# Residual norms: squares summed as moving columns into one row, in place of token-column products

## The chip, the cores and the metric

One Trainium2 chip, of which the kernel uses one core. The metric is device time in microseconds (us) of one execution. The engines are TensorE (PE in the views; PEld is its weight load), VectorE (DVE), ScalarE (ACT), GpSimd (POOL) and SyncE (SP), which issues the DMAs. Each runs its own instruction stream, and they are ordered by semaphores.

## The reference, cut to what matters

Two blocks of two layers each work on a residual stream x of width 1024, with 512 latent tokens and, in the first block's first layer, 256 context tokens beside them. Each layer part starts with an RMS norm over the 1024 channels of a token:

```
def rmsnorm(x, g):
    xf = x.astype(jnp.float32)
    y = xf * lax.rsqrt(jnp.mean(xf * xf, axis=-1, keepdims=True) + EPS)
    return (y * g).astype(x.dtype)

xl = xl + ml[2] * rmsnorm(yl, norm_mix_post[layer])
hl = modulate(rmsnorm(xl, norm_ffn_pre[layer]), ml[3], ml[4])
xl = xl + ml[5] * rmsnorm(conv_ffn(hl, ...), norm_ffn_post[layer])
```

The sum of squares of x for the second line is what is computed in another way here. The mixers (gated recurrences, mLSTM, gated delta rule), the convolutions and the feed-forward products stay as they are.

## The kernel before

x is held with the channels on the 128 partitions, as eight parts `xT[:, k, :]` of up to 768 token columns (256 context, then 512 latent; `LATENT` stands for the latter alone, `BOTH` for the two segments). A sum over channels is therefore a sum over partitions, which TensorE makes.

Each engine's stream is written by hand, in the order in which it runs; semaphores (`signal(...)`) tie the streams together. Around one residual norm this happens:

- VectorE (`add_normed_dve`, L553) scales the branch output y and adds it to x, part by part: L558 and L561 alternate.
- ScalarE (`x_square_act`, L530) squares each finished part of x into `hT` (L533).
- TensorE (`x_norm_pe`, L518) waits for a square and calls `token_sums_pe` (L493): for each group c of 128 tokens the 128x128 square is the stationary operand and one column of ones moves (L497). The result is one PSUM column of 128 tokens for each k, 48 columns for six groups.
- VectorE (`norm_roots_dve`, L542) reduces the eight columns of a group to one (L547), scales and adds EPS (L548); ScalarE takes the root (L528); VectorE inverts (L550).
- TensorE (`norm_spread_pe`, L501) spreads the columns over all partitions with an identity product (L505), into `RT` in PSUM.
- VectorE multiplies x by `RT` (L569, in the delta layer L2581), ScalarE makes the high part of the split operand (L581 or L2404), VectorE the low part (L572), and the next weight products (L357, L1815) start.

The columns of y's norm are made by the same `token_sums_pe`, with n = 2, and are not touched. `x_norm_pe` is called in four places: before the first feed-forward block and before the mLSTM block (BOTH, six groups), before the second feed-forward block and before the first delta block (LATENT, four groups). The second delta layer and the final norm make their sums with `x_sum_pe` inside `join_pe`; these stay.

Two other things are queued at these places. At the first two POOL starts splitting weight blocks into high and low parts (L327, L328) once VectorE has added the last part of x. At the last two ScalarE and VectorE split blocks themselves (L1840, L1845), which stand in VectorE's stream ahead of the norm; before the mLSTM block VectorE has the modulation vectors (L706 to L708) there.

Of the kernel before, what the change touches and what calls it, by code (L numbers as in the profile page):

```python
# [9 lines left out]
ALU = mybir.AluOpType  # L10
ACT = mybir.ActivationFunctionType
AX = mybir.AxisListType.X

P = 128
D = 1024
KD = D // P
# [4 lines left out]
EPS = 1e-6  # L21
# [127 lines left out]
def program(nc, A, out):  # L149

    with ExitStack() as ctx:
        build(nc, A, out, ctx)

def build(nc, A, out, ctx):
    SIGNALS.clear()
    V, S, G, M = nc.vector, nc.scalar, nc.gpsimd, nc.tensor

    def signal(name):
        q = Signal(ctx.enter_context(nc.semaphore(name)))  # L160
        q.label = name
        SIGNALS.append(q)
        return q
# [26 lines left out]
    hT = h_all[:, :].rearrange("p (k t) -> p k t", k=KD)  # L190
    hlT = h_low[:, :].rearrange("p (k t) -> p k t", k=KD)
    ones, ident, halves, ident64 = gen[:, 0:P], gen[:, P:2 * P], gen[:, 2 * P:3 * P], gen[:, 3 * P:3 * P + 64]
# [35 lines left out]
    psum = [banks[:, 512 * i:512 * i + 512] for i in range(8)]  # L228
# [12 lines left out]
    def cols(name, at=0, n=1):  # L241
        return vec[:, COL[name] + at:COL[name] + at + n]

    BOTH = [(0, CTX), (CTX, LAT)]
    LATENT = [(CTX, LAT)]
# [13 lines left out]
    sum_ready = signal("sums_ready")  # L259
    ms_ready = signal("mean_squares_ready")  # L260
# [3 lines left out]
    dve_step = signal("dve_step")  # L264
# [17 lines left out]
    def link(e, step, ins):  # L282

        ins.then_inc(step.sem, 1)
        e.wait_ge(step)
# [200 lines left out]
    x_squared, cols_ready, rt_spread = signal("x_squared"), signal("norm_columns_ready"), signal("norm_spread")  # L486
# [3 lines left out]
    def extent(segs):  # L490
        return segs[0][0], segs[-1][0] + segs[-1][1]

    def token_sums_pe(pe, k, n, t, segs):  # L493

        lo, hi = extent(segs)
        for c in range(lo // P, hi // P):
            ins = M.matmul(psum[4][:, n * c + k:n * c + k + 1], t[:, P * c:P * c + P], ones[:, 0:1], start=True, stop=True)  # L497
        if k == n - 1:
            ins.then_inc(sum_ready.sem, 1)

    def norm_spread_pe(pe, segs):  # L501
        lo, hi = extent(segs)
        pe.wait_ge(cols_ready)
        for c in range(lo // P, hi // P):
            ins = M.matmul(RT[:, P * c:P * c + P], norm_cols[:, c:c + 1].to_broadcast([P, P]), ident, start=True, stop=True)  # L505
        ins.then_inc(rt_spread.sem, 1)
# [7 lines left out]
    def x_sum_pe(pe, k, segs):  # L514
        pe.wait_ge(x_squared)
        token_sums_pe(pe, k, KD, hT[:, k, :], segs)

    def x_norm_pe(pe, segs):  # L518
        for k in range(KD):
            x_sum_pe(pe, k, segs)  # L520
        norm_spread_pe(pe, segs)

    def norm_root_act(act, segs):
        lo, hi = extent(segs)
        S.activation(spare, ones[:, 0:1], ACT.Sqrt)
        act.wait_ge(ms_ready)
        t = norm_cols[:, lo // P:hi // P]
        S.activation(t, t, ACT.Sqrt).then_inc(root_ready.sem, 1)  # L528
# [6 lines left out]
    def x_norm_act(act, segs, between=None):  # L535
# [3 lines left out]
            between()  # L539
        norm_root_act(act, segs)  # L540

    def norm_roots_dve(dve, segs, n):  # L542
        lo, hi = extent(segs)
        a, b = lo // P, hi // P
        t = norm_cols[:, a:b]
        dve.wait_ge(sum_ready)
        link(dve, dve_step, V.tensor_reduce(t, psum[4][:, n * a:n * b].rearrange("p (c k) -> p c k", k=n), AX, ALU.add))  # L547
        V.tensor_scalar(t, t, 1.0 / D, EPS, ALU.mult, ALU.add).then_inc(ms_ready.sem, 1)  # L548
        dve.wait_ge(root_ready)
        V.reciprocal(t, t).then_inc(cols_ready.sem, 1)  # L550
        dve.wait_ge(rt_spread)
# [11 lines left out]

    def prenorm_split_dve(dve, segs, high):
        lo, hi = extent(segs)
        norm_roots_dve(dve, segs, KD)
        for k in range(KD + 1):
            if k < KD:
                V.tensor_tensor(hT[:, k, lo:hi], xT[:, k, lo:hi], RT[:, lo:hi], ALU.mult).then_inc(scaled.sem, 1)  # L569
            if k:  # L570
                dve.wait_ge(to_dve)
                V.tensor_tensor(hlT[:, k - 1, lo:hi], hT[:, k - 1, lo:hi], high[:, k - 1, lo:hi].bitcast(F32),  # L572
                                ALU.subtract).then_inc(h_ready.sem, 1)
# [2001 lines left out]
        val_used.skip(act, 2)  # L2575

    def delta_prenorm_dve(dve, l):
        norm_roots_dve(dve, LATENT, KD)
        for k in range(KD + 1):
            if k < KD:  # L2580
                V.scalar_tensor_tensor(hT[:, k, CTX:T], xT[:, k, CTX:T], cols("norm_w", 8 * l + k), RT[:, CTX:T],  # L2581
                                       ALU.mult, ALU.mult).then_inc(to_act.sem, 1)
            if k:
                dve.wait_ge(to_dve)
                V.tensor_tensor(hl_d[:, k - 1, :], hT[:, k - 1, CTX:T], hh_d[:, k - 1, :].bitcast(F32), ALU.subtract)                    .then_inc(h_ready.sem, 1)  # L2585
# [736 lines left out]
    def _(e):  # L3322
# [17 lines left out]
        phase(pe)  # L3340
        norm_spread_pe(pe, BOTH)
        x_norm_pe(pe, BOTH)
        ffn_pe(pe, 0, BOTH)
        full_down_pe(pe)
# [275 lines left out]
```

## Time and profile before

| | us |
|---|---|
| median of 3 runs | 3460.76 |
| lowest, highest | 3458.69, 3464.58 |
| the profiled execution | 3454.87 |
| its span | 3453.1 |
| PE busy | 3150.2 (91%) |
| PE weight loads busy | 2617.6 (76%) |
| DVE busy | 1926.2 (56%) |
| ACT busy | 1170.8 (34%) |
| POOL busy | 319.7 (9%) |

The page of the profile gives busy times and the costliest groups.
### The profile page before, as it was taken

The page shows a single profiled execution, that of the slowest core. Times are in us where ns is not written, and L with a number is a line of the kernel's source. Part 1 is how long each engine was busy: PE and PEld are TensorE (multiplying, and loading weights), DVE is VectorE, ACT ScalarE, POOL GpSimd, SP SyncE. Part 2 cuts the span into 40 slices and gives each one's busy share as a digit, 9 for nine tenths or more (in the row PEclk, how much of TensorE's full clock was granted, in tenths as well). Part 3 has the DMA queues.
Part 4 walks back from the last instruction along what each step waited for, and adds up shares of the span by engine and source line. Part 5 has one row for each costly group of instructions (what it writes and reads, how often), then busy time and mean ns, then how long its engine had stood idle before and what let it go on. Part 6 is the DMA issues. An engine that isn't in the chain of part 4 may idle for free. (4 is left out here: it accounts for less than half of the span.)

```text
span 3453.1 us, 69128 instructions
## 1 busy us (share of the span) xinstructions
PE 3150.2 (91%) x30200; PEld 2617.6 (76%) x30200; DVE 1926.2 (56%) x3106; ACT 1170.8 (34%) x2171; POOL 319.7 (9%) x196
## 2 busy tenths in 40 slices
PE   4999799978999989988897899999988999988898
PEld 1777488867888877776796788787777777878777
DVE  3134645453677741243278588625766854766854
ACT  2111344434222231223333433324435243525442
POOL 1232000001344400032000000000000000000000
PEclk6999899987999999889798899998989999989999
DMA  7563000020111111111000122231210222210122
GB/s 265 186 231 115 2 4 5 5 81 31 61 61 61 67 55 61 54 41 63 1 1 7 57 96 93 90 104 62 74 38 4 74 92 75 80 50 4 56 86 80
DMA packets 62760, 230.30 MB, mean 67 GB/s; under 512 B 7456, under 2 KB 7968, under 8 KB 62240
## 3 DMA queue, kind: packets, MB, share of 16 engines
q1 hardware_dynamic: 62496, 226.36, 19.0%
q8 instruction: 217, 3.56, 0.4%
q14 instruction: 47, 0.39, 0.0%
HBM read 224.24 MB, written 2.10 MB: 66 GB/s over the span
## 5 line engine op out<-in xcount | busy, mean ns | idle before, releaser
L1787 DVE SCALAR_TENSOR_TENSOR arena<-arena,vec 128x512 f32<-128x512 f32 (+1 forms) x220 | 203.3, 941 | 25.5 <-DVE arena L1785 0.2
L357 PE MATMUL bank<-h_high_ffn,w_high_ffn 128*128 128x256 f32 x704 | 183.4, 343 | 9.6 <-DVE h_low L572 9.4
L2425 DVE SCALAR_TENSOR_TENSOR x_all<-arena,vec,x_all 128x512 f32<-128x512 f32 x240 | 180.0, 750 | 10.4 <-ACT arena L2535 3.7
L357 PE MATMUL bank<-h_low,w_high_ffn 128*128 128x256 f32 x704 | 181.8, 340 | 0.0
L1845 DVE TENSOR_TENSOR ring_low<-ring,w_high_ffn 128x1024 fp32r<-128x1024 f32 x84 | 102.5, 1224 | 141.4 <-ACT w_high_ffn L1840 138.4
L357 PE MATMUL bank<-h_high_ffn,ring_low 128*128 128x256 f32 x704 | 179.9, 336 | 0.0
L357 PE MATMUL bank<-h_high_d,w_high_d 128*128 128x512 f32 x384 | 156.9, 409 | 6.4 <-DVE h_low_d L2585 6.4
L357 PE MATMUL bank<-h_low_d,w_high_d 128*128 128x512 f32 x384 | 152.9, 398 | 0.0
L357 PE MATMUL bank<-h_high_d,ring_low 128*128 128x512 f32 x384 | 152.5, 397 | 0.0
L357 PEld LDWEIGHTS bank<-h_high_ffn,w_high_ffn 128*128 128x128 f32 x704 | 132.4, 189 | 26.4 <-DVE h_low L572 7.5
L1897 DVE SCALAR_TENSOR_TENSOR arena<-arena,vec 128x512 f32<-128x512 f32 x176 | 132.4, 752 | 30.7 <-ACT arena L1858 25.3
L357 PEld LDWEIGHTS bank<-h_low,w_high_ffn 128*128 128x128 f32 x704 | 135.1, 192 | 14.8
L1815 PE MATMUL bank<-h_high_ffn,w_high_ffn 128*128 128x512 f32 x352 | 140.9, 400 | 4.9 <-DVE h_low L572 4.9
L357 PEld LDWEIGHTS bank<-h_high_ffn,ring_low 128*128 128x128 f32 x704 | 133.3, 189 | 15.4
L357 PE MATMUL bank<-h_high_b,w_high_b 128*128 128x512 f32 x320 | 130.6, 408 | 10.3 <-DVE h_low L3122 5.2
L1845 DVE TENSOR_TENSOR ring_low<-ring,w_high_b 128x1024 fp32r<-128x1024 f32 x72 | 87.9, 1223 | 92.7 <-ACT w_high_b L1840 92.4
L1817 PE MATMUL bank<-h_high_ffn,ring_low 128*128 128x512 f32 x352 | 139.6, 397 | 0.0
L1816 PE MATMUL bank<-h_low,w_high_ffn 128*128 128x512 f32 x352 | 139.1, 395 | 0.0
L357 PE MATMUL bank<-h_high_b,ring_low 128*128 128x512 f32 x320 | 128.0, 400 | 0.0
L357 PE MATMUL bank<-h_low,w_high_b 128*128 128x512 f32 x320 | 127.4, 398 | 0.0
L1840 ACT ACTIVATE w_high_ffn<-ring 128x1024 fp32r<-128x1024 f32 x84 | 88.3, 1056 | 114.0 <-DMA ring<-in_ffn_down_dram 111.9
L1350 DVE COPY_PREDICATED x_all<-arena,bank 128x256 f32<-128x256 uint32 x120 | 53.5, 446 | 128.0 <-PE bank L1104 128.0
(572 smaller groups left out, 8070.4 us busy)
## 6 DMA issues: line engine op xcount, KB each, us to landing
arena<-in_ada_w_dram SPq DMA_DIRECT2D x96, 512.0 KB, 5.5
ring<-in_ffn_up_dram SPq DMA_DIRECT2D x88, 512.0 KB, 3.3
ring<-in_d_branch_dram SPq DMA_DIRECT2D x56, 512.0 KB, 3.3
ring<-in_ffn_down_dram SPq DMA_DIRECT2D x48, 512.0 KB, 3.3
ring<-in_d_in_dram SPq DMA_DIRECT2D x32, 512.0 KB, 3.3
ring<-in_ab_in_dram SPq DMA_DIRECT2D x19, 512.0 KB, 7.2
ring<-in_c_in_dram SPq DMA_DIRECT2D x17, 512.0 KB, 3.3
ring<-in_d_join_dram SPq DMA_DIRECT2D x16, 512.0 KB, 3.3
```

The costliest lines, as they stand in the source:

```text
L357: ins = M.matmul(bank_of(tile % 2, seg), w[:, at], x(k, seg), start=first, stop=last)
L1350: V.copy_predicated(X[:, 2 * s:2 * s + 2].rearrange("p j h t -> p h j t"), level_mask[lv].unsqueeze(1).unsqueeze(1).to_broadcast([P, 2, 2, ...
L1787: ins = V.scalar_tensor_tensor(y, a, w(dy, dx), y, ALU.mult, ALU.add)
L1815: M.matmul(bank, wh[:, at], xh, start=k == 0, stop=False)
L1816: M.matmul(bank, wh[:, at], xl, start=False, stop=False)
L1817: ins = M.matmul(bank, wl[:, at], xh, start=False, stop=k == KD - 1)
L1840: S.activation(high[slot], ring[slot][:, :], ACT.Identity).then_inc(w_high_ready.sem, 1)
L1845: V.tensor_tensor(ring_low[slot][:, :], ring[slot][:, :], high[slot].bitcast(F32), ALU.subtract)\
L1897: ins = V.scalar_tensor_tensor(y, grid_at(t % 2, dy, dx), cols("ffn_conv", KF * (9 + 3 * dy + dx) + t), y, ALU.mult, ALU.add)
L2425: ins = V.scalar_tensor_tensor(y, halves2(cpad[i][:, tap:tap + LAT]), w, y, ALU.mult, ALU.add)
```

## The change

In `x_norm_pe` the square becomes the moving operand. The stationary operand is one column of ones, so the result is one row of up to 768 sums on partition 0, accumulated in PSUM over the eight parts: 256 context columns in bank 4, 512 latent columns in bank 5. VectorE copies this row into SBUF (`x_row`, partition 0 of the first square, which is no longer needed). TensorE then turns it to token columns: for each group of 128 tokens one product with the 1x128 piece of the row as stationary operand and a single 1 moving. `norm_roots_dve` is called with n = 1, so that the reduction over k falls away and the scaling reads PSUM. This adds two semaphore steps: VectorE waits for the row sums before the copy, and TensorE waits for the copy.

```
     def x_norm_pe(pe, segs):
+        lo, hi = extent(segs)
         for k in range(KD):
-            x_sum_pe(pe, k, segs)
+            pe.wait_ge(x_squared)
+            for seg in segs:
+                ins = M.matmul(x_row_banks(seg), ones[:, 0:1], hT[:, k, seg[0]:seg[0] + seg[1]], start=k == 0, stop=k == KD - 1)
+        ins.then_inc(sum_ready.sem, 1)
+        pe.wait_ge(row_ready)
+        for c in range(lo // P, hi // P):
+            ins = M.matmul(psum[4][:, c:c + 1], x_row[:, P * c:P * c + P], ones[0:1, 0:1], start=True, stop=True)
+        ins.then_inc(sum_ready.sem, 1)
         norm_spread_pe(pe, segs)
...
+    def x_row_dve(dve, segs):
+        dve.wait_ge(sum_ready)
+        for seg in segs:
+            ins = V.tensor_copy(x_row[:, seg[0]:seg[0] + seg[1]], x_row_banks(seg))
+        ins.then_inc(row_ready.sem, 1)
...
-        link(dve, dve_step, V.tensor_reduce(t, psum[4][:, n * a:n * b].rearrange("p (c k) -> p c k", k=n), AX, ALU.add))
-        V.tensor_scalar(t, t, 1.0 / D, EPS, ALU.mult, ALU.add).then_inc(ms_ready.sem, 1)
+        sums = psum[4][:, n * a:n * b]
+        if n > 1:
+            link(dve, dve_step, V.tensor_reduce(t, sums.rearrange("p (c k) -> p c k", k=n), AX, ALU.add))
+            sums = t
+        V.tensor_scalar(t, sums, 1.0 / D, EPS, ALU.mult, ALU.add).then_inc(ms_ready.sem, 1)
...
     def prenorm_split_dve(dve, segs, high):
         lo, hi = extent(segs)
-        norm_roots_dve(dve, segs, KD)
+        x_row_dve(dve, segs)
+        norm_roots_dve(dve, segs, 1)
...
     def delta_prenorm_dve(dve, l):
-        norm_roots_dve(dve, LATENT, KD)
+        if not l:
+            x_row_dve(dve, LATENT)
+        norm_roots_dve(dve, LATENT, KD if l else 1)
```

TensorE's stream before the first feed-forward block, as it was (out<-in, then the output's shape and how many in a row; `gen` holds the ones and the identity, `h_all` the squares):

```order
L497 MATMUL bank<-gen,arena 128x1 x12
L505 MATMUL bank<-gen,small 128x128 x6
L497 MATMUL bank<-gen,h_all 128x1 x48
L505 MATMUL bank<-gen,small 128x128 x6
L357 MATMUL bank<-h_high_ffn,w_high_ffn 128x256
```

And as it is with the change; a pair of 256 and 512 columns stands eight times (L527 are the row sums, L531 the turn to columns):

```order
L497 MATMUL bank<-gen,arena 128x1 x12
L505 MATMUL bank<-gen,small 128x128 x6
L527 MATMUL bank<-h_all,gen 1x256
L527 MATMUL bank<-h_all,gen 1x512
...
L527 MATMUL bank<-h_all,gen 1x256
L527 MATMUL bank<-h_all,gen 1x512
L531 MATMUL bank<-gen,h_all 128x1 x6
L505 MATMUL bank<-gen,small 128x128 x6
L357 MATMUL bank<-h_high_ffn,w_high_ffn 128x256
```

48 products with one moving column became 16 with 256 or 512, and six with one column stand behind them, after the wait for the copy.

VectorE's stream before the second feed-forward block, as it was (L1845 are the low parts of two weight blocks):

```order
L561 TENSOR_TENSOR x_all<-x_all,arena 128x512 x2
L1845 TENSOR_TENSOR ring_low<-ring,w_high_ffn 128x1024 x2
L547 TENSOR_REDUCE small<-bank 128x4
L548 TENSOR_SCALAR small<-small 128x4
L550 RECIPROCAL small<-small 128x4
L569 TENSOR_TENSOR h_all<-x_all,bank 128x512 x2
```

And with the change, where the same lines have other numbers (L582, L1867, L569, L571, L591) and L557 is the copy:

```order
L582 TENSOR_TENSOR x_all<-x_all,arena 128x512 x2
L1867 TENSOR_TENSOR ring_low<-ring,w_high_ffn 128x1024 x2
L557 COPY h_all<-bank 1x512
L569 TENSOR_SCALAR small<-bank 128x4
L571 RECIPROCAL small<-small 128x4
L591 TENSOR_TENSOR h_all<-x_all,bank 128x512 x2
```

The reduction is gone, and the copy, for which TensorE now waits, stands behind the weight splits.

## Rows read from the trace of the kernel before

**Rows 1.** Timeline, place A: start us, us, engine line op out<-in [idle before<-releaser]

```profile
821.06 20.64 PE L497 MATMUL bank<-gen,h_all 128*128 128x1 f32 x96 [3.65 <-ACT h_all L533]
...
830.56 1.71 ACT L533 ACTIVATE h_all<-x_all 128x768 f32<-128x768 f32 x2 [0.89 <-DVE x_all L561]
...
841.61 1.05 POOL L327 TENSOR_SCALAR w_high_ffn<-ring 128x1024 fp32r<-128x1024 f32 x1
841.73 0.21 DVE L547 TENSOR_REDUCE small<-bank 128x6 f32<-128x48 f32 x1 [10.33 <-PE bank L497]
841.98 0.71 DVE L548 TENSOR_SCALAR small<-small 128x6 f32<-128x6 f32 x1
...
843.21 2.93 PE L505 MATMUL bank<-gen,small 128*128 128x128 f32 x12 [1.51 <-DVE small L550]
846.18 1.82 DVE L569 TENSOR_TENSOR h_all<-x_all,bank 128x768 f32<-128x768 f32 x2 [3.02 <-PE bank L505]
```

**Rows 2.** Timeline, place B, before the mLSTM block

```profile
1451.44 20.64 PE L497 MATMUL bank<-gen,h_all 128*128 128x1 f32 x96 [3.65 <-ACT h_all L533]
...
1465.18 1.02 DVE L708 TENSOR_TENSOR modv<-mods,vec 128x16 f32<-128x16 f32 x1
...
1476.60 1.82 DVE L569 TENSOR_TENSOR h_all<-x_all,bank 128x768 f32<-128x768 f32 x2 [3.02 <-PE bank L505]
```

**Rows 3.** Timeline, place C, before the second feed-forward block

```profile
1941.63 13.81 PE L497 MATMUL bank<-gen,h_all 128*128 128x1 f32 x64 [2.64 <-ACT h_all L533]
...
1950.35 2.36 DVE L1845 TENSOR_TENSOR ring_low<-ring,w_high_ffn 128x1024 fp32r<-128x1024 f32 x2 [1.64 <-ACT w_high_ffn L1840]
...
1955.70 0.17 DVE L548 TENSOR_SCALAR small<-small 128x4 f32<-128x4 f32 x1
...
1956.38 2.08 PE L505 MATMUL bank<-gen,small 128*128 128x128 f32 x8 [0.94 <-DVE small L550]
1958.49 1.29 DVE L569 TENSOR_TENSOR h_all<-x_all,bank 128x512 f32<-128x512 f32 x2 [2.17 <-PE bank L505]
```

**Rows 4.** Timeline, place D, before the first delta block

```profile
2350.26 13.82 PE L497 MATMUL bank<-gen,h_all 128*128 128x1 f32 x64 [2.64 <-ACT h_all L533]
...
2358.99 1.23 DVE L1845 TENSOR_TENSOR ring_low<-ring,w_high_d 128x1024 fp32r<-128x1024 f32 x1 [1.65 <-ACT w_high_d L1840]
...
2367.13 1.41 DVE L2581 SCALAR_TENSOR_TENSOR h_all<-x_all,vec,bank 128x512 f32<-128x512 f32 x2 [2.17 <-PE bank L505]
```

**Rows 5.** Windows: busy us (records) of each engine, then PEclk, DMA share, GB/s

```profile
821.00:841.70 20.70, 20.64 (x96) 20.55 (x96) 10.40 (x12) 6.00 (x9) 11.53 (x7) 0.50 0.00 0
...
851.00:857.00 6.00, 5.85 (x17) 4.25 (x18) 4.29 (x6) 6.00 (x11) 0.00 (x0) 0.50 0.01 3
857.00:863.00 6.00, 3.40 (x17) 2.28 (x16) 4.85 (x6) 6.00 (x11) 0.00 (x0) 1.00 0.00 0
```

**Rows 6.** Timeline of the program's first norm (L468), products and weight loads

```profile
14.46 11.95 PE L468 MATMUL bank<-h_all,gen 128*128 128x256 f32 x32 [14.46 <-ACT h_all L458]
...
15.45 1.92 PE L468 MATMUL bank<-h_all,gen 128*128 128x512 f32 x2
...
19.37 0.19 PEld L468 LDWEIGHTS bank<-h_all,gen 128*128 128x128 f32 x1 [0.24 <-issue]
...
20.66 0.19 PEld L468 LDWEIGHTS bank<-h_all,gen 128*128 128x128 f32 x1 [0.24 <-issue]
```

**Rows 7.** Timeline and source lines: small products, spreads, a PSUM read

```profile
811.39 2.73 PE L497 MATMUL bank<-gen,arena 128*128 128x1 f32 x24
...
815.21 2.19 PE L505 MATMUL bank<-gen,small 128*128 128x128 f32 x12 [1.09 <-DVE small L550]
...
1444.89 2.90 PE L505 MATMUL bank<-gen,small 128*128 128x128 f32 x12 [1.34 <-DVE small L550]
...
26.45 1.02 DVE L475 TENSOR_SCALAR arena<-bank 128x256 f32<-128x256 f32 x2 [12.71 <-PE bank L468]
...
L2022 PEld LDWEIGHTS bank<-gen,arena x48: 285/330/335, 1679.0 to 1689.0; 64*128 64x128 f32 x48
```

More of the change, by code:

```diff
@@ L516, in x_sum_pe @@
         token_sums_pe(pe, k, KD, hT[:, k, :], segs)
+    x_row_banks = lambda seg: psum[4][0:1, 256:256 + seg[1]] if seg[0] == 0 else psum[5][0:1, 0:seg[1]]
+    x_row = hT[0:1, 0, :]
+    row_ready = signal("norm_row_ready")
     def x_norm_pe(pe, segs):
+        lo, hi = extent(segs)
         for k in range(KD):
-            x_sum_pe(pe, k, segs)
+            pe.wait_ge(x_squared)
[6 more added lines that the diff above has]
+        ins.then_inc(sum_ready.sem, 1)
         norm_spread_pe(pe, segs)
```

## The prediction

> **What bounds the kernel now.** The change touches only the sum of squares of the residual rows in four places, so I read those four places in the timeline, in order of time, and ask at each what the first use of the finished norm waits for. I call them A (before the first feed-forward block), B (before the mLSTM block), C (before the second feed-forward block) and D (before the first delta block). A and B work on all 768 token columns, C and D on 512.
>
> At A [rows 1] ScalarE squares eight parts of x; the last two squares start at 830.56 and end at 832.27 us. TensorE takes the first square at 821.06 and is busy for 20.64 us, to 841.70, with 96 records. In this trace an f32 product stands as two records, so these are 48 token-column products. TensorE thus ends 9.4 us after its last input. VectorE starts its reduction at 841.73, and the first multiplication with the finished norm starts at 846.18. So TensorE is what ends last at A, not the adds on VectorE or the squares. B is the same picture: 20.64 us from 1451.44, first use at 1476.60 [rows 2]. C takes 13.81 us from 1941.63, to 1955.44 (first use 1958.49) [rows 3], D 13.82 us from 2350.26, to 2364.08 (first use 2367.13) [rows 4].
>
> The reason is in the granted clock. Through 821 to 841.7 it is 0.50, that is the 1.2 GHz level, though TensorE is busy without a break [rows 5]. 20.64 us over 96 records is 0.215 us a record and 2.58 us a part of six products. The squares come faster: TensorE takes the first at 821.06 and the seventh ends at 831.41, six steps of 1.73 us. At full clock the same kind of product costs 2.73/24 = 0.114 us a record [rows 7].
>
> **The change, part by part.**
>
> *Sums.* Per part of 768 columns six products with a 128-column weight load and one moving column go; two products with 256 and 512 moving columns and one stationary column come. No row has one stationary column. The nearest one is the first norm of the program, which streams the same squares, 256 and 512 columns, through a 128-column matrix of ones [rows 6]. A part starts each 20.66 − 19.37 = 1.29 us there, at the full clock; at half of it 2.58 us, and two 512-column records, two thirds of a part, did take 1.92 us with their drain at the start (15.45). A smaller weight load can only take off what shows of loads, which is little where the loads run beneath the products, so I take both figures as they are; for 512 columns 1.72 and 0.86 us.
>
> So at the low clock nothing is gained: 2.58 us both ways. All of it hangs on whether the clock comes back while the row sums run. Before it rose, TensorE did this: in the first norm, some 3 us of these streaming products (32 records took 11.95 us where eight parts of 1.29 are 10.3; 1.6 us too long is 3.3 us at half speed); and 6 us of split products with 256 and 512 columns, from 851 to 857 [rows 5, 6]. It did not rise for the one-column products at A (20.64 us), nor at B, C and D, nor for 10 us of small products from 1679.0 to 1689.0, whose weight loads took 0.33 us in the median against 0.19 us at full clock [rows 6, 7]. The new products are of the first kind in what they stream. I take 4.5 us, the middle of 3 and 6.
>
> At A then: 4.5 us at 2.58 is 1.7 parts, the other 6.3 parts at 1.29 need 8.1 us, which gives 833.7; but the last two squares end at 831.41 and 832.27, and two parts behind the first of these give 834.0. With 6 us: 2.3 parts, then 5.7 × 1.29 = 7.3, so 834.4. The sum ends at 834.0 to 834.4 instead of 841.70. At B, by the same offsets, at 1464.4; but VectorE is in the modulation vectors until 1466.20 [rows 2], so its copy starts there. At C: 4.5 us is 2.6 parts, 5.4 × 0.86 more gives 1950.8 (with 6 us 1951.5), and VectorE has two weight splits ahead of the copy, to 1950.35 + 2.36 = 1952.71 [rows 3]. At D 2359.4 (2360.1), VectorE free at 2358.99 + 1.23 = 2360.22 [rows 4]. So at B, C and D what is late next is VectorE's own queue, and at A it is the squares.
>
> *The row to columns.* New on the path behind the sums: VectorE copies 256 and 512 elements of one partition (a pair of PSUM reads of that length took 1.02 us [rows 7]; I take 1.02, and two thirds, 0.68, for 512 alone), TensorE makes six (four) small products, and a reduction of 0.21 us goes. The small products load 128 columns of one row each. The nearest rows are the one-column products of 128 rows, 0.215 us a record at the low clock and 0.114 at the full one; those of 64 rows are no cheaper (48 records from 1679.0 to 1689.0 are 0.21 us each). So 12 records are 1.4 to 2.7 us with the drain, 8 records 0.95 to 1.8 us.
>
> *The root.* From the scaling on VectorE to the first spreading product 0.68 us (1955.70 to 1956.38 [rows 3]). At A and B the scaling took 0.71 us where it takes 0.17 at C: it ended with the POOL operation of 841.61 to 842.66, while the reduction before it, which reads PSUM, took 0.21 beside the same operation [rows 1]. The new scaling reads PSUM, so I take 0.17, which gives back 0.54 us each at A and B. The Trainium skill, VectorE: DVE Perf Modes, section Why PSUM operands drop a tier, says that a PSUM operand keeps an instruction out of the mode that uses both SBUF read ports; by it the new scaling and the copies would have no port to wait for, and the trace agrees as far as the 0.21 us beside 0.71 goes.
>
> *The spread.* Unchanged work: 2.19 us at full clock (815.21), 2.93 at the low one (843.21), 2.08 us for eight records at the low one [rows 1, 3, 7].
>
> Handing over costs about 0.04 us each. From the start of the copy to the first use, all at the low clock: A and B 1.06 + 2.7 + 0.68 + 2.93 + 0.04 = 7.4 us; C and D 0.72 + 1.8 + 0.04 + 0.68 + 2.08 + 0.04 = 5.36 us. All at the full clock: A, B 5.4 us; C, D 0.72 + 0.95 + 0.72 + 1.46 (8/12 of 2.19) + 0.04 = 3.9 us. Which level: after a pause of 1.3 us the spread ran at full clock at 815.21, and at the low one at 1444.89 (2.90 us) [rows 7]. At A only the copy lies between, so I take the small products at full and the spread at the low clock, 6.2 us; at B, C and D TensorE has been idle for two to three microseconds, so the low one.
>
> - A: 834.1 + 6.2 = 840.3 against 846.18: 5.9 gained (4.4 to 6.8).
> - B: 1466.2 + 7.4 = 1473.6 against 1476.60: 3.0 (to 5.0).
> - C: 1952.71 + 5.36 = 1958.1 against 1958.49: 0.4 (to 1.9).
> - D: 2360.22 + 5.36 = 2365.6 against 2367.13: 1.5 (to 3.0).
>
> Sum 10.8 us, ends 9.3 and 16.7. Behind the first use everything is paced by the same VectorE and ScalarE steps as before, then by TensorE, so it passes on whole. POOL's splits are not moved: they start with a signal that the change leaves where it is, and the last of four is under way at 841.61, ahead of the products that need it. No DMA is moved. The new wait of TensorE for the copied row has only the small products and the spread behind it, which need it anyway.
>
> The profiled execution took 3454.87 us (span 3453.1), 5.9 below the median 3460.76 of the runs. The gain is a difference of stretches, so I take it off the median: 3450.0 us.
>
> **The rivals.**
>
> *Slower: the clock stays low under the row sums.* One stationary column is something no row shows, and the one-column products show that a busy TensorE alone is not enough. Then the sums end where they end now (eight parts at 2.58 are 20.6 us), and the copy and the small products come on top: A 841.7 + 7.4 = 849.1, 3.0 later; B 1472.1 + 7.4 = 1479.5, 2.9 later; C 1955.44 + 5.4 = 1960.8, 2.3 later; D 2364.08 + 5.4 = 2369.5, 2.3 later: 10.5 us lost, 3471.3. Where it decides: with r us at the low clock the sums at A end at 821.06 + 10.32 + r/2, and A breaks even at 838.8, that is for r near 15. Against it: both streaming stretches had the full clock within some 6 us. 0.18.
>
> *Level: back at A and B only, or delayed by POOL.* C and D have shorter stretches. If the clock rises only at A and B, 8.9 − 4.6 = 4.3 us are gained, 3456.5. Or the copies do wait for POOL: a VectorE operation on 128x16 elements took 1.02 us at 1465.18 while POOL was splitting [rows 2], and three such waits at A and B, 0.9 us each, take 5.4 us of the 10.8, 3455.4. 0.12.
>
> *The change does nothing here* would need the sums to be off the path. At A they end 9.4 us after the last square and the next instruction starts 0.03 us later; I leave nothing for it.
>
> **How the numbers follow.** Forecast 0.70, level 0.12, slower 0.18. Within 0.2% is within 6.9 us, about what a measurement of this kernel can tell from no change. The forecast's ends, 9.3 and 16.7, are both beyond it: faster 0.70, same 0.12, slower 0.18. The range goes from 3443 (all at the full clock, 3444.1) to 3461 (the level cases and the runs' own spread of 3 us); left out is the slower case, 0.18.
>
> **What would show each step.** The row sums at A end near 834, with granted clock 1.00 before 828; parts 1.29 us apart or waiting for a square afterwards. At B the copy starts at 1466 less what A gained, at C directly behind the two weight splits. The two copies take about 1 us, the 12 small records 1.4 to 2.7 us, the scaling 0.17 us. Wrong if the clock is 0.50 to the end of the sums, if the small products take over 3 us, or if the copies last as long as POOL's operations beside them.

## The result, and the profile after

| | us | ratio to before (95% interval) |
|---|---|---|
| before, median of 4 runs beside it | 3459.73 (3456.08 to 3464.58) | |
| with the change, median of 4 runs | 3436.96 (3433.41 to 3438.49) | 0.9935 (0.9922 to 0.9947) |
| forecast | 3450.0 (3443 to 3461) | |

The change made the kernel faster by 22.8 us in this comparison. The direction and the mechanism are those of the forecast; the size is not: 10.8 us were forecast, and the time fell below the range. Two later comparisons of the same two kernels, with more runs, gave 0.9951 (0.9938 to 0.9965) and 0.9943 (0.9925 to 0.9962). The runs of before that stood beside others and those with the change (72 and 18 over all comparisons) have medians of 3457.4 and 3437.9 us and means of 3456.85 and 3438.15 us: about 18.7 us. The 0.9935 of the first comparison lies just outside the interval of the second and inside that of the third.

The page of the profile after the change, its first line and its busy times (of the whole execution, each engine's share of the span in brackets):

```profile
span 3435.7 us, 68762 instructions
PE 3125.1 (91%) x30016; PEld 2554.7 (74%) x30016; DVE 1926.3 (56%) x3108; ACT 1171.0 (34%) x2171; POOL 320.7 (9%) x196
```

TensorE is busy 25 us less than in the table of before and its weight loads 63 us less; the other engines are as before. Now the places. At A, the answer to [rows 1], in the timeline (start us, us, engine line op out<-in, and in brackets the idle time before it and what ended it):

```profile
826.49 6.78 PE L527 MATMUL bank<-h_all,gen 128*1 128x256 f32 x16 [3.66 <-ACT h_all L545]
...
833.42 1.45 PE L527 MATMUL bank<-h_all,gen 128*1 128x256 f32 x4 [0.15 <-ACT h_all L545]
...
835.99 1.71 ACT L545 ACTIVATE h_all<-x_all 128x768 f32<-128x768 f32 x2 [0.89 <-DVE x_all L582]
836.89 2.74 PE L527 MATMUL bank<-h_all,gen 128*1 128x256 f32 x8 [0.28 <-ACT h_all L545]
...
839.67 1.01 DVE L557 COPY h_all<-bank 1x256 f32<-1x256 f32 x2 [2.84 <-PE bank L527]
840.12 1.04 POOL L327 TENSOR_SCALAR w_high_ffn<-ring 128x1024 fp32r<-128x1024 f32 x1
...
840.73 1.49 PE L531 MATMUL bank<-gen,h_all 1*128 1x1 f32 x12 [1.10 <-DVE h_all L557]
...
842.26 0.16 DVE L569 TENSOR_SCALAR small<-bank 128x6 f32<-128x6 f32 x1 [1.59 <-PE bank L531]
...
842.95 2.80 PE L505 MATMUL bank<-gen,small 128*128 128x128 f32 x12 [0.72 <-DVE small L571]
...
845.78 1.82 DVE L591 TENSOR_TENSOR h_all<-x_all,bank 128x768 f32<-128x768 f32 x2 [2.89 <-PE bank L505]
```

Windows of the same stretch (each engine's busy us and records in the order PE, PEld, DVE, ACT, POOL, then PEclk), beside [rows 5]:

```profile
826.50:829.00 2.50, 2.50 (x4) 0.41 (x5) 2.50 (x4) 0.84 (x1) 0.00 (x0) 0.50 0.00 0
829.00:830.00 1.00, 1.00 (x4) 0.32 (x3) 1.00 (x3) 0.84 (x1) 0.00 (x0) 0.77 0.00 0
830.00:832.00 2.00, 2.00 (x7) 0.50 (x6) 2.00 (x3) 0.84 (x1) 0.00 (x0) 1.00 0.00 0
...
842.00:844.00 2.00, 1.28 (x8) 1.20 (x8) 0.36 (x2) 0.21 (x1) 2.00 (x2) 0.78 0.00 0
844.00:846.00 2.00, 1.75 (x9) 1.45 (x7) 0.22 (x1) 0.00 (x0) 1.92 (x2) 0.50 0.00 0
```

Read them together. The row sums start at the low clock, and within 829 to 830 the granted clock goes to 1.00, 3.0 us after their start. Over the four places and three profiled executions it rose 2.9 to 5.5 us after the start, latest at C (4.1 to 5.5 us). From 833.42 on TensorE waits for each square ("<-ACT h_all L545") and needs 1.45 us, with its drain, for a part that comes every 1.73 us. It ends at 839.63, which is 1.93 us behind the last square (835.99 + 1.71 = 837.70) instead of 9.4. In the brackets the releaser of TensorE has become ScalarE: that is what "the bound has moved" looks like in a timeline.

Places B, C and D, the answers to [rows 2], [rows 3] and [rows 4]; first B:

```profile
1465.40 1.00 DVE L557 COPY h_all<-bank 1x256 f32<-1x256 f32 x2
...
1466.45 1.55 PE L531 MATMUL bank<-gen,h_all 1*128 1x1 f32 x12 [2.59 <-DVE h_all L557]
1467.86 1.04 POOL L327 TENSOR_SCALAR w_high_m<-ring 128x1024 fp32r<-128x1024 f32 x1
1468.04 0.17 DVE L569 TENSOR_SCALAR small<-bank 128x6 f32<-128x6 f32 x1 [1.64 <-PE bank L531]
...
1468.73 2.93 PE L505 MATMUL bank<-gen,small 128*128 128x128 f32 x12 [0.72 <-DVE small L571]
```

C, where the copy stands behind two weight splits:

```profile
1934.67 9.08 PE L527 MATMUL bank<-h_all,gen 128*1 128x512 f32 x16 [2.64 <-ACT h_all L545]
...
1943.40 2.36 DVE L1867 TENSOR_TENSOR ring_low<-ring,w_high_ffn 128x1024 fp32r<-128x1024 f32 x2 [1.64 <-ACT w_high_ffn L1862]
...
1945.68 0.67 DVE L557 COPY h_all<-bank 1x512 f32<-1x512 f32 x1
...
1946.40 1.05 PE L531 MATMUL bank<-gen,h_all 1*128 1x1 f32 x8 [2.65 <-DVE h_all L557]
...
1948.16 1.30 PE L505 MATMUL bank<-gen,small 128*128 128x128 f32 x8 [0.71 <-DVE small L571]
1949.49 1.29 DVE L591 TENSOR_TENSOR h_all<-x_all,bank 128x512 f32<-128x512 f32 x2 [1.39 <-PE bank L505]
```

And D:

```profile
2349.99 0.67 DVE L557 COPY h_all<-bank 1x512 f32<-1x512 f32 x1
2350.71 1.05 PE L531 MATMUL bank<-gen,h_all 1*128 1x1 f32 x8 [1.17 <-DVE h_all L557]
...
2352.47 2.08 PE L505 MATMUL bank<-gen,small 128*128 128x128 f32 x8 [0.71 <-DVE small L571]
```

None of the three copies has an idle time in brackets: VectorE had no pause before them, it came to them from its own queue. TensorE had then been idle for 2.59, 2.65 and 1.17 us.

From here on I measure every profiled execution in the same way. The stretch of a norm runs from the start of the first sum on TensorE to VectorE's first use of the finished norm (where unused products hold up the first sum, from where it would start, 0.05 us behind the end of the first square); "rest" is the span without the four stretches.

| kernel (profiled span) | A | B | C | D | four together | rest |
|---|---|---|---|---|---|---|
| before (3453.1) | 25.12 | 25.15 | 16.87 | 16.87 | 84.0 | 3369.1 |
| before, again (3452.7) | 25.06 | 25.11 | 16.87 | 16.87 | 83.9 | 3368.8 |
| with the change (3435.7) | 19.29 | 20.96 | 14.82 | 14.47 | 69.5 | 3366.2 |
| with the change, again (3437.4) | 18.59 | 21.37 | 15.97 | 14.69 | 70.6 | 3366.8 |
| with the change, third (3438.1) | 18.29 | 21.22 | 15.93 | 14.62 | 70.1 | 3368.0 |

So the four stretches gave 13.4 to 14.5 us in three executions. That is the part which the change explains directly.

### The profile page after: what moved, and what is told of

It reads as the page before. It is cut to its first block and busy times, and to the rows that moved or that the text cites. A ratio compares the mean times of both kernels' runs of the same rounds, so it can differ in the third digit from the quotient of the medians.

```text
span 3435.7 us, 68762 instructions
## 1 busy us (share of the span) xinstructions
PE 3125.1 (91%) x30016; PEld 2554.7 (74%) x30016; DVE 1926.3 (56%) x3108; ACT 1171.0 (34%) x2171; POOL 320.7 (9%) x196
## 5 line engine op out<-in xcount | busy, mean ns | idle before, releaser
L357 PE MATMUL bank<-h_high_ffn,w_high_ffn 128*128 128x256 f32 x704 | 178.9, 335 | 10.8 <-DVE h_low L594 10.6
L1867 DVE TENSOR_TENSOR ring_low<-ring,w_high_ffn 128x1024 fp32r<-128x1024 f32 x84 | 102.6, 1224 | 142.1 <-ACT w_high_ffn L1862 139.2
L1867 DVE TENSOR_TENSOR ring_low<-ring,w_high_b 128x1024 fp32r<-128x1024 f32 x72 | 87.9, 1223 | 92.8 <-ACT w_high_b L1862 92.4
```

Source lines behind the costliest of these rows:

```text
L357: ins = M.matmul(bank_of(tile % 2, seg), w[:, at], x(k, seg), start=first, stop=last)
L1867: V.tensor_tensor(ring_low[slot][:, :], ring[slot][:, :], high[slot].bitcast(F32), ALU.subtract)\
```

## Experiments: how much, and where

**The kernel before once more**, as a measure of what two identical kernels differ by.

> The kernel before, unchanged, to see how far two of its executions differ stage by stage. Theory 1 (the whole gain arises inside the four norm stretches, 14.5 us by the two traces; the other 8 us between the medians are differences from one execution to the next): ratio 1.000 within 0.2%, and the untouched stretches, above all the one from the first use at D to the end (1086.0 us before, 1081.1 after), wander by several us here too. Theory 2 (the change also shortens untouched stretches, by what it does to the clock behind it): this stretch stays within 1 us of 1086.0.

Measured: 3457.71 us (median of 10) beside 3456.62 (29), ratio 1.0007 (0.9996 to 1.0017). The stretch from the first use at D to the end took 1080.4 us, where the first execution of before had 1086.0 and the one with the change 1081.1: the untouched stretch wanders by itself, as theory 1 has it.

**The changed kernel once more.**

> The changed kernel once more. Both theories: the four stretches from the first sum to the first use are 19.3, 21.0, 14.8 and 14.5 us within 0.7 us each. Theory 1: some 14.5 us below the kernel before, 3444 to 3446 us where the kernel before is at 3459. Theory 2: 20 to 25 us below, with the stretch from D to the end at 1081 again.

Measured: 3438.71 (8 runs) beside 3456.62, ratio 0.9951 (0.9938 to 0.9965), that is 16.9 us (12 to 21). The 22.8 us of the first comparison do not come back in full, and by time alone neither theory falls. The stretch at C was 16.0 us, outside the 0.7 us that I had allowed around 14.8.

**The change at A and B alone.** C and D keep the token-column products:

```
-    def x_norm_pe(pe, segs):
+    def x_norm_pe(pe, segs, row=True):
         lo, hi = extent(segs)
+        if not row:
+            for k in range(KD):
+                x_sum_pe(pe, k, segs)
+            norm_spread_pe(pe, segs)
+            return
...
-        x_norm_pe(pe, LATENT)
+        x_norm_pe(pe, LATENT, False)
```

> Row sums at A and B only, token-column products at C and D. Theory 1: 10.0 us below the kernel before (5.8 at A, 4.2 at B). Theory 2: 10 us in the two stretches and a part of the further 8 us, 12 to 16 us in all, the more the nearer the untouched stretch lies to A and B.

Measured: 3444.33 (10), ratio 0.9968 (0.9956 to 0.9980), 11.1 us (7 to 15). Stretches: A 18.38, B 21.26, C 16.86, D 16.87, together 10.5 us below before.

**At C and D alone**, the same edit with `x_norm_pe(pe, BOTH, False)`.

> Row sums at C and D only. Theory 1: 4.4 us below the kernel before (2.0 at C, 2.4 at D). Theory 2: 4.4 us and what C and D hand on, above all from D to the end (4.9 us by the two traces): 8 to 12 us.

Measured: 3449.75 (10), ratio 0.9984 (0.9973 to 0.9995), 5.5 us (2 to 9). Stretches: A 25.08, B 25.11, C 14.73, D 14.67, together 4.3 us below before.

What follows: the two halves give 11.1 and 5.5 us, together 16.6, and the whole gave 16.9 in the same comparison. Within these wide intervals the gain is made place by place, and nothing asks for an effect that needs all four. The stretches of C and D give more (4.3 us) than the forecast's 1.9 us.

## Experiments: what brings the clock back

Two theories. Mine: the moving columns. Streaming 256 and 512 columns brings the clock back, however wide the stationary operand is; products that move one column neither bring it back nor keep it. The rival: TensorE starts these sums cold in any case, and any work that had warmed it would have done the same for the old products.

**A wide stationary operand.** The row sums with all 128 columns of ones, into 128 PSUM rows of which one is used:

```
-                ins = M.matmul(x_row_banks(seg), ones[:, 0:1], hT[:, k, seg[0]:seg[0] + seg[1]], start=k == 0, stop=k == KD - 1)
+                ins = M.matmul(x_row_banks(seg), ones, hT[:, k, seg[0]:seg[0] + seg[1]], start=k == 0, stop=k == KD - 1)
```

> The changed kernel with all 128 columns of ones as the stationary operand of the row sums, so that the row of sums appears on all partitions of PSUM; the copy still takes one. Theory (the clock rises because of what is streamed, however wide the stationary operand is): sums at A end 13.1 to 13.4 us after the first one starts, as with one column (13.14), C and D 9.1 to 9.7, and the four stretches sum to 70 to 71 us. Rival (one stationary column makes the clock rise late or the products cheaper): the low-clock time at A differs from the changed kernel's by over 2 us, or a part at the full clock is not 1.29 us.

Measured: a single run of 3441.36, beside 3457.02 (23 runs), so no ratio; stretches 19.07, 21.48, 15.96, 14.47. Its timeline and a window at A:

```profile
826.47 8.49 PE L527 MATMUL bank<-h_all,gen 128*128 128x256 f32 x20 [3.65 <-ACT h_all L545]
...
836.87 2.85 PE L527 MATMUL bank<-h_all,gen 128*128 128x256 f32 x8 [0.18 <-ACT h_all L545]
```

```profile
829.00:831.00 2.00, 2.00 (x6) 1.21 (x5) 2.00 (x4) 1.07 (x2) 0.00 (x0) 0.77 0.00 0
831.00:833.00 2.00, 2.00 (x9) 1.18 (x7) 2.00 (x3) 1.11 (x2) 0.00 (x0) 1.00 0.00 0
```

The sums at A take 13.25 us from first start to last end, against 13.14; a pair of parts 2.85 us against 2.74. The width of the stationary operand buys nearly nothing. The forecast's price, taken from the 128-column products of [rows 6], was right for that reason.

**The old products, behind a warm clock.** The kernel before, with three products of 448 moving columns ahead of each norm, in TensorE's idle time before the first square. They read `gen` and write a bank that nobody reads; nothing of the computation is left out.

```
     def x_norm_pe(pe, segs):
+        for _ in range(3):
+            M.matmul(psum[5][0:1, 0:448], ones[:, 0:1], gen[:, 0:448], start=True, stop=True)
         for k in range(KD):
             x_sum_pe(pe, k, segs)
```

> Token-column products as in the kernel before, but ahead of them, in the pause after the spread of y's norm, three f32 products of one stationary column with 448 moving columns each, read from constants and used by nobody (4.5 us at the low clock, so the first sum starts up to 1 us later). Theory (what was slow before was only the clock, and the streamed products raise it, but column products do not hold it): the sums at A take part of their time at the full clock and then fall back, 14 to 18 us instead of 20.6; 5 to 12 us gained in all. Rival (the column products are slow for another reason than the clock): still 20.6 us of sums and a time about 2 us above the kernel before.

Measured: 3449.86 (10) beside 3457.02, ratio 0.9980 (0.9968 to 0.9991), 7.2 us by the medians, within the 5 to 12 expected; stretches 24.05, 24.11, 15.66, 14.81, together 5.4 us below before (at C the unused products end 1.3 us after the first square is ready, which the 15.66 contain). Timeline at A, with one line from C, and windows at A:

```profile
827.49 1.50 PE L497 MATMUL bank<-gen,h_all 128*128 128x1 f32 x12 [1.19 <-ACT h_all L537]
829.22 1.50 PE L497 MATMUL bank<-gen,h_all 128*128 128x1 f32 x12 [0.23 <-ACT h_all L537]
830.95 15.52 PE L497 MATMUL bank<-gen,h_all 128*128 128x1 f32 x72 [0.23 <-ACT h_all L537]
...
1944.19 11.27 PE L497 MATMUL bank<-gen,h_all 128*128 128x1 f32 x64
```

```profile
827.00:829.00 2.00, 1.50 (x12) 1.41 (x12) 2.00 (x3) 1.11 (x2) 0.00 (x0) 1.00 0.00 0
829.00:831.00 2.00, 1.55 (x13) 1.47 (x13) 2.00 (x4) 1.01 (x2) 0.00 (x0) 0.97 0.00 0
831.00:833.00 2.00, 2.00 (x10) 2.00 (x10) 2.00 (x3) 0.84 (x1) 0.00 (x0) 0.50 0.00 0
```

This is the sharpest reading of the study. At full clock a part of old products takes 1.50 us and keeps pace with the squares (0.23 us idle before each). Two parts later the clock is 0.50, and the remaining 72 records take 15.52 us without a break. The short waits are not what brings the clock down: at C the 64 records follow the unused products without any, and the granted clock is 0.75 from 1944 to 1950 and 0.50 behind; and the row sums with a warm start, further below, wait 0.28 us before nearly every part and keep the full clock. The sums at A take 18.98 us (14 to 18 were expected) instead of 20.64: of the 7.5 us by which the row sums are shorter, a warm start gives the old products 1.7. What the row sums have and these have not is that the clock stays up beneath them. One thing these kernels do not separate: under the old products the weight loads fill the time (busy 20.55 of 20.70 us [rows 5]), so whether the few moving columns or the time spent in loads is what counts, no run here tells.

**Fillers between the parts**, to hold the clock under the old products: the same three leading products, and one of 128 moving columns behind each of the first seven parts.

```
             x_sum_pe(pe, k, segs)
+            if k < KD - 1:
+                M.matmul(psum[5][0:1, 0:128], ones[:, 0:1], gen[:, 0:128], start=True, stop=True)
```

> The same, and behind each part but the last one more unused product with 128 moving columns. Theory: if these are enough to hold the full clock, a part is 1.37 + 0.22 us, under the 1.73 us at which squares arrive at A and B, the sums at A end about 1.4 us after the last square, and neither the copy nor the turn to columns is needed: A 17 us from first square to first use (19.3 in the changed kernel), C and D 13 to 14; 18 to 22 us below the kernel before. If they do not hold it: between e2_cols_lead and the kernel before. Rival: no gain over the kernel before.

Measured: 3461.25 (10), ratio 1.0010 (0.9997 to 1.0023); stretches 27.5, 27.5, 20.2, 17.3, together 8.5 us above before. A miss. At A in its timeline:

```profile
825.79 1.50 PE L497 MATMUL bank<-gen,h_all 128*128 128x1 f32 x12
827.22 0.38 PE L524 MATMUL bank<-gen 128*1 128x128 f32 x2
827.53 2.72 PE L497 MATMUL bank<-gen,h_all 128*128 128x1 f32 x12
830.18 0.59 PE L524 MATMUL bank<-gen 128*1 128x128 f32 x2
```

The third part is at half speed in spite of the fillers, though TensorE has not paused since the first, and the fillers then cost 0.52 us each at that clock.

**Wider fillers**, 256 moving columns in place of 128.

> The same with 256 moving columns behind each part but the last. Theory: holds the full clock if 128 columns do not, but a part is 1.37 + 0.43 = 1.80 us, slightly over the pace of the squares at A and B, and 0.91 + 0.43 = 1.34 over the 1.20 at C and D: 1 to 2 us later at each place than a clean 128-column case, 15 to 20 us below the kernel before. Rival: the time is at or above that of the kernel before.

Measured: 3473.03 (8), ratio 1.0047 (1.0030 to 1.0063), slower by 16 us: a miss too. In its profile at A two parts take 1.50 us and six take 2.72, with 1.01 us of filler between. What follows: some streaming between the old products is not enough to hold the clock; both my expectations on fillers are refuted. With the row sums, which stream all the time, it holds.

## Experiments: what is late next

With the sums ended early, the trace shows VectorE's own queue in front of the copy at B, C and D. These kernels ask what each remaining piece is worth. They ran beside the changed kernel and 16 runs of before (3459.28 us).

**The changed kernel, third time.**

> The changed kernel a third time, with more runs. Theory 1 (the gain arises in the four stretches, 13.4 to 14.5 us by two traces each): 14 to 16 us below the kernel before. Theory 2 (something outside the stretches is systematic): 18 to 23 us, as the first comparison had it.

Measured: 3438.02 (6), ratio 0.9943 (0.9925 to 0.9962), that is 19.7 us (13 to 26): in the middle of theory 2's range, with theory 1's inside the interval. Time alone does not decide between them; the part on the prediction comes back to it.

**A warm start for the row sums**, three unused products of 448 columns ahead of them:

```
     def x_norm_pe(pe, segs, fill_rows=1):
         lo, hi = extent(segs)
+        for _ in range(3):
+            unused_pe(448)
```

> The changed kernel with three unused f32 products of 448 moving columns ahead of the row sums at each place, so that the clock is up from the first square on. Theory (the sums now end where the squares and VectorE let them, the clock's rise is hidden): the sums at A end within 0.3 us of where they did (13.1 us after the first), and the time equals the changed kernel's within 3 us. Rival (the low-clock microseconds at the start still cost): 1.5 to 3 us less at each of C and D, 5 us faster in all.

Measured: 3442.39 (9), ratio 0.9952 (0.9937 to 0.9967), 4.4 us above the changed kernel by the medians where 3 were allowed, with intervals that overlap; stretches 18.08, 21.16, 15.93, 14.63. At A:

```profile
825.02 1.45 PE L532 MATMUL bank<-h_all,gen 128*1 128x256 f32 x4 [0.28 <-ACT h_all L554]
...
833.69 2.74 PE L532 MATMUL bank<-h_all,gen 128*1 128x256 f32 x8 [0.28 <-ACT h_all L554]
```

Nearly every part now waits 0.28 us for its square, and the sums still take 13.13 us. At A the first 3 us at the low clock cost the changed kernel nothing, since TensorE catches up before the last square: nothing is left to gain in these sums. The 5 us of the rival did not come either.

**VectorE's work moved behind the copy.** At B half of the modulation vectors, at C the two weight splits, at D the one split go into the gaps in which TensorE works:

```
         x_row_dve(dve, segs)
-        norm_roots_dve(dve, segs, 1)
+        if turning:
+            turning()
+        norm_roots_dve(dve, segs, 1, spreading)
...
-        modv_dve(dve, 1)
-        prenorm_split_dve(dve, BOTH, hh_m)
+        modv_dve(dve, 1, (0,))
+        prenorm_split_dve(dve, BOTH, hh_m, None, lambda: modv_dve(dve, 1, (1,)))
...
-        for i in range(2):
-            split_low_dve(dve, block_starts["ffn", 1] + i, wh_ffn)
-        prenorm_split_dve(dve, LATENT, hh_ffn)
+        low = lambda i: lambda: split_low_dve(dve, block_starts["ffn", 1] + i, wh_ffn)
+        prenorm_split_dve(dve, LATENT, hh_ffn, low(0), low(1))
...
             x_row_dve(dve, LATENT)
+            split_low_dve(dve, block_starts["delta", 0], wh_d)
...
-            split_low_dve(dve, block_starts["delta", l], wh_d)
+            if l:
+                split_low_dve(dve, block_starts["delta", l], wh_d)
```

> The changed kernel with VectorE's other work moved behind the copy: at B half of the modulation vectors is made while TensorE spreads, at C one weight split while TensorE turns the row and one while it spreads, at D the split while it turns the row. Theory (at B, C and D VectorE's queue is what is late): the copies start when the sums end, 1.0 to 1.5 us earlier at B, 1.5 to 1.9 at C, 0.3 to 0.5 at D, less 0.3 each where a moved step is longer than the pause it fills; 2 to 3.5 us below the changed kernel. Rival (the moved work only delays what comes behind): no difference or 1 us slower.

Measured: 3434.88 (6), ratio 0.9940 (0.9917 to 0.9962); stretches 18.56, 19.31, 12.88, 14.16, together 64.9 against 70.1. At C:

```profile
1942.26 0.68 DVE L566 COPY h_all<-bank 1x512 f32<-1x512 f32 x1 [2.11 <-PE bank L532]
...
1942.87 1.20 DVE L1880 TENSOR_TENSOR ring_low<-ring,w_high_ffn 128x1024 fp32r<-128x1024 f32 x1
1943.00 1.05 PE L538 MATMUL bank<-gen,h_all 1*128 1x1 f32 x8 [0.77 <-DVE h_all L566]
1944.08 0.16 DVE L578 TENSOR_SCALAR small<-bank 128x4 f32<-128x4 f32 x1
```

The copy now waits for TensorE ("<-PE bank L532") and not for the queue, and each split hides under the small products or the spread. C is 3.0 us shorter than in the third run of the changed kernel, B 1.9; the 5.2 us together are more than the 2 to 3.5 expected.

**The same, with unused products of 256 columns in TensorE's two pauses**, behind the row sums and behind the small products:

```
         ins.then_inc(sum_ready.sem, 1)
+        for _ in range(2 if segs is BOTH else 1):
+            unused_pe(256)
         pe.wait_ge(row_ready)
...
         ins.then_inc(sum_ready.sem, 1)
+        unused_pe(256)
         norm_spread_pe(pe, segs)
```

> The same order, and unused products (f32, 256 moving columns) in TensorE's pauses: two at A and B and one at C and D while VectorE copies, and one while the root is taken. Theory (the small products and the spread behind pauses run at the low clock in part, 2.93 us at B against 2.19, 2.08 at D against 1.3): the spreads come down to 2.2 and 1.3 us at most places, 1.5 to 3 us below the kernel with the order alone, 4 to 6 us below the changed kernel. Rival: the fillers do not keep the clock up, or lie on the path: no difference or up to 2 us slower.

Measured: 3433.22 (6), ratio 0.9939 (0.9918 to 0.9961); stretches 18.10, 19.22, 13.35, 13.00, together 63.7. At D:

```profile
2339.58 1.05 PE L538 MATMUL bank<-gen,h_all 1*128 1x1 f32 x8 [0.34 <-DVE h_all L566]
2340.56 0.59 PE L523 MATMUL bank<-gen 128*1 128x256 f32 x2
2341.33 1.16 PE L505 MATMUL bank<-gen,small 128*128 128x128 f32 x8 [0.18 <-DVE small L580]
```

The spread at D takes 1.16 us instead of 2.08, at full clock; at B it still takes 2.73. Against the kernel with the order alone D is 1.2 us shorter, A 0.5, B 0.1, and C 0.5 us longer, so most of the 1.5 to 3 us expected is not there. The last two kernels are 5.2 and 6.4 us shorter in their stretches than the changed kernel, and 3.1 and 4.8 us by the medians. The intervals of the three ratios overlap almost wholly, so by time alone neither is proven faster than the changed kernel.

## Why the prediction was right in its mechanism and wrong in its size

**Right: which engine, and what the row sums do to the clock.** The sums at A end 13.14 us after their start, where 13.0 to 13.3 were forecast. The granted clock was back 2.9 to 5.5 us after the start, around the 4.5 us that were taken, and the warm start shows that at A this does not matter. At B, C and D the copies start 14.68, 11.01 and 9.88 us after the first sum (forecast 14.76, 11.08, 9.96), behind VectorE's queue, as said; the reordered kernel confirms that this queue is what held them.

**Right: the prices of the copy and the scaling.** The copies take 1.01, 1.00 and 0.67 us (1.02 and 0.68), the scaling 0.16 and 0.17 us at A and B (0.17 forecast), at B beside the POOL operation of 1.04 us that starts at 1467.86; before, it took 0.71 beside such an operation at A [rows 1]. The Trainium skill, VectorE: DVE Perf Modes, section Why PSUM operands drop a tier, says that an operand in PSUM keeps an instruction out of the mode that reads through both SBUF ports. The trace agrees with what the prediction drew from it: no instruction of the new path that reads PSUM waited for POOL, also not the copies at A and B (1.01 and 1.00 us with POOL busy beside them). The rivals fell: the clock did not stay low, and C and D gained too.

**Wrong, first: the clock level of the small products.** The failing step is "at B, C and D TensorE has been idle for two to three microseconds, so the low one". I inferred the level from one pair of spreads behind pauses of 1.09 and 1.34 us [rows 7], of which one was faster and one slow, and settled on the slow one. The small products began at the full level in all four places and in all three executions, behind 1.10 us of idleness at A, 2.6 at B, 2.0 to 2.7 at C and 1.2 to 1.4 at D. At A they kept it to the end each time. At B, C and D they kept it in the first execution (but for the last quarter of a microsecond at B), and in the other two the clock fell while they ran:

| | taken | measured, three executions |
|---|---|---|
| small products at B | 2.7 | 1.55, 1.96, 1.80 |
| at C | 1.8 | 1.05, 1.42, 1.38 |
| at D | 1.8 | 1.05, 1.27, 1.20 |
| spread at A | 2.93 | 2.80, 2.10, 1.80 |
| at C | 2.08 | 1.30, 2.07, 2.08 |

The three values of a row are the three executions, in the order of the table of stretches. These terms were mis-sized by 2.65, 1.65 and 1.92 us for the small products, and by 0.9, 0.8 and 1.1 us for the spreads at A and C. Added to 10.8 they give 14.4, 13.3 and 13.8 us for the stretches; 14.5, 13.4 and 13.9 were measured. The spread at B took 2.93 and at D 2.07 to 2.08 each time, as forecast. So the levels were right in kind (they do fall behind the pauses) and taken a few microseconds too early. The windows at A show it for the spread: 0.78 from 842 to 844, 0.50 after.

One reading behind the levels was wrong too. The spread at 815.21, which I took for one at full clock behind 1.3 us, stands behind 1.09 us and ran at full clock for a third of its time only:

```profile
815.20:816.00 0.80, 0.79 (x7) 0.80 (x8) 0.00 (x0) 0.00 (x0) 0.00 (x0) 0.99 0.00 0
816.00:817.40 1.40, 1.40 (x8) 1.11 (x6) 0.00 (x0) 0.00 (x0) 0.00 (x0) 0.50 0.04 12
```

At full clock throughout, twelve records take 1.60 us (A with the warm start, clock 1.00) and eight take 1.13 (from 1937.86 in the kernel before, clock 0.99), not 2.19 and 1.46. So the sum "all at the full clock" should have been about 1.9 us more, 18.6 us or some 3442 us, still above what was measured.

| gained, us | A | B | C | D | sum |
|---|---|---|---|---|---|
| forecast | 5.9 | 3.0 | 0.4 | 1.5 | 10.8 |
| measured, three executions | 5.8, 6.5, 6.8 | 4.2, 3.8, 3.9 | 2.0, 0.9, 0.9 | 2.4, 2.2, 2.2 | 14.5, 13.4, 13.9 |

**Wrong, second: from the stretches to the whole.** "I take it off the median" and "it passes on whole" allow nothing beside the stretches, and the range ended one microsecond below the sum of the most favourable levels. The whole gained about 18.7 us, of which 13.9 are in the stretches. The 13.0 us between forecast and measured time are thus made up of four pieces: 3.1 in the stretches, 4.8 outside them over all runs, 4.1 that only the first comparison shows, which I put down to chance, and 1.0 because the forecast was taken from 3460.76 and not from 3459.73. Where the 4.8 us lie I cannot show. What the runs say: the mean time of all runs is 18.7 us shorter, but the mean span of the profiled executions only 15.9 us (3452.9 to 3437.1), because the two profiled ones of before were 2.2 us faster than before is on average, and the three with the change 0.7 slower. Outside the stretches the profiled ones differ by 2.0 us, and that is less than what chance does there: the 800 us ahead of A, which no part of the change precedes, took 821.1 and 829.5 us in the two executions of before, and the rest of the span lies anywhere from 3362.0 to 3377.8 us over the fourteen profiled executions of this study (3377.8 with the change at A and B alone). In favour of a real effect: the mean granted clock of the runs (0.9365 before, 0.9462 with the change) amounts to some 69 us less at the low level, and the stretches account for 56 of these. Against it: the low-clock time outside the stretches in the profiled executions is 352 and 347 us before, 332, 345 and 359 us with the change, and in the 30 us behind each norm it is no shorter (39 and 40 us before; 38, 42 and 43 after). And the halves: A and B alone gained about as much as their stretches did (11.1 and 10.5 us), as far as an interval of 7 to 15 us can say. The cause of these 4.8 us stays open.

**The range.** Even with the right level of the small products the time would have been put at some 3447, inside the range: the first failing step alone does not bring the time out of it. The true range had to hold what a comparison of a few runs adds: the same kernel before ran from 3446.7 to 3465.6 us in 72 runs, and its medians in the comparisons from 3456.6 to 3459.7, while I had taken 3 us, half the width of the three runs before me (3458.69 to 3464.58).

## What to carry to other kernels

Look for TensorE work that is busy without a break and still at a granted clock of 0.50; products that move one column are such work, and turning them round so that the long side moves brought the sums at A from 20.64 to 13.14 us, most of it at the full clock, although the count of columns moved rose from 48 to 6144. Once such a stretch is short, read who releases the next step: here three of four places then waited for VectorE's queue, and moving work that nobody needs yet behind the new copy shortened the stretches by another 5 us in the profiled execution, though the time of the whole does not prove it. Where a small term's price hangs on a clock level behind a pause, keep both levels and give the range both, and let the range be as wide as many runs scatter, not as three do.

## What the runs showed of the hardware that I had not expected

- A full clock is lost under products that move one column: with the leading products it goes from 0.97 (829 to 831) to 0.50 (831 to 833) behind two parts, and it does so at C as well, where TensorE does not pause. The Trainium skill, TensorE: Matmul & The Clock Gate, Part 1, The HAM clock gate, has the gate follow how busy TensorE has recently been; in this trace engine-busy time is not that measure (20.64 us at 0.50 with no idle time [rows 1, 5]), while under the row sums, with 256 and 512 moving columns, the clock rose at all four places in all three executions.
- One product of 128 or 256 moving columns behind every twelve such records did not hold it either.
- Behind a pause of 1.2 to 2.7 us after the row sums the next products still began at full speed (eight records in 1.05 to 1.42 us, against the 1.8 estimated for the low clock), and the spread that followed a second pause of 0.7 us was mostly slow at B and D (2.93 and 2.07 to 2.08 us in all three executions).
- The loads of one stationary column are short, and those of one row by 128 columns are not. The line of each load in the profile of the changed kernel (least, median and greatest duration in ns):

```profile
L527 PEld LDWEIGHTS bank<-h_all,gen x96: 79/84/126, 826.5 to 2348.5; 128*1 128x1 f32 x96
...
L531 PEld LDWEIGHTS bank<-gen,h_all x40: 181/187/243, 840.7 to 2351.5; 1*128 1x128 f32 x40
```

One row of 128 columns costs 187 ns in the median, as 128 rows do at full clock in [rows 6] (0.19 us), and 128 rows of one column 84 ns: in these loads the columns decide, not the rows.
